# Expert loop of a two-block transformer: the down projection as three products of rounded halves

## The reference, cut to what matters

```
def expert_block(args):
    tok_b, w_b, e = args
    xb = h[tok_b]                                            # 128 x 1024
    hid = jax.nn.silu(xb @ w_e_gate[e]) * (xb @ w_e_up[e])   # 128 x 256
    return (hid @ w_e_down[e]) * w_b[:, None].astype(h.dtype)  # 128 x 1024
```

## Time and profile before

| | |
|---|---|
| median of 3 runs | 3463.89 us (3462.14 to 3467.74) |
| the profiled execution | 3471.0 us, of which its span is 3469.1 us |
| mean granted TensorE clock | 0.978 |
| busy over the span | PE 95%, PEld 74%, DVE 47%, ACT 42%, POOL 38% |
| share of the chain that ended last | PE 79%, DVE 5%, DMA 5%, ACT 4%, issue 4% |

### The profile page before, as it was taken

One profiled execution on the slowest core, in us unless ns is written; L12 is line 12 of the kernel. 1 busy time (PEld: TensorE's weight loads), 2 busy tenths in 40 slices (PEclk: granted clock), 3 DMA queues, 4 the chain that ended last, 5 costly groups with the idle time before them and its releaser, 6 DMA issues.

```text
span 3469.1 us, 44440 instructions
## 1 busy us (share of the span) xinstructions
PE 3280.9 (95%) x17062; PEld 2582.8 (74%) x17062; DVE 1633.8 (47%) x2252; ACT 1455.0 (42%) x1859; POOL 1325.3 (38%) x1076
## 2 busy tenths in 40 slices
PE   7999997899889999999879999998999998899999
PEld 4788886678556666666567888887888877678887
DVE  4555448455576666666543544545311132452121
ACT  4344435522435555555444555555322242342221
POOL 2323137444213333333335444432444443344444
PEclk9999999999999999999989999999999999999999
DMA  5211110244259999999833222221322212032222
GB/s 213 63 50 62 37 49 13 73 178 177 84 205 341 348 343 349 374 359 363 327 121 98 86 80 87 90 86 61 110 97 97 97 50 72 13 109 97 97 97 73
DMA packets 98532, 496.87 MB, mean 143 GB/s; under 512 B 22447, under 2 KB 22703, under 8 KB 49729
## 3 DMA queue, kind: packets, MB, share of 16 engines
q1 hardware_dynamic: 78480, 454.86, 36.8%
q0 software_dynamic: 19888, 39.73, 3.2%
HBM read 472.48 MB, written 40.89 MB: 148 GB/s over the span
## 4 chain that ended last, share of the span: by engine, by line
PE 79%; DVE 5%; DMA 5%; ACT 4%; issue 4%; POOL 2%; SPq 1%; POOLq 0%; ACTq 0%; DVEq 0%
PE ps L283 13%; PE ps L284 13%; PE ps L285 13%; PE ps L2072 7%; DMA arena<-we_gu 4%; PE ps L289 4%; PE ps L291 3%; PE ps L290 3%; PE ps L2057 2%; PE ps L2061 2%; PE ps L2060 2%; PE ps L2610 1%; PE ps L2598 1%; PE ps L705 1%; PE ps L2580 1%
## 5 line engine op out<-in xcount | busy, mean ns | idle before, releaser
L283 PE MATMUL ps<-arena_r,arena_r 128*128 128x512 f32 x2080 | 826.0, 397 | 22.8 <-POOL ring_r L273 6.9
L284 PE MATMUL ps<-arena_r,arena_r 128*128 128x512 f32 x2080 | 815.1, 392 | 0.0
L273 POOL TENSOR_TENSOR ring_r<-ring,arena_r 128x512 fp32r<-128x512 f32 x400 | 554.6, 1418 | 654.3 <-ACT arena_r L268 654.3
L268 ACT ACTIVATE arena_r<-ring 128x2048 fp32r<-128x2048 f32 x166 | 316.7, 1909 | 408.7 <-PE ps L285 331.4
L273 POOL TENSOR_TENSOR arena_r<-ring,arena_r 128x512 fp32r<-128x512 f32 x264 | 335.3, 1302 | 381.0 <-ACT arena_r L268 381.0
L283 PEld LDWEIGHTS ps<-arena_r,arena_r 128*128 128x128 f32 x2080 | 393.2, 189 | 115.2 <-issue 22.6
L284 PEld LDWEIGHTS ps<-arena_r,arena_r 128*128 128x128 f32 x2080 | 393.7, 189 | 81.5 <-issue 1.9
L285 PE MATMUL ps<-arena_r,arena_r 128*128 128x512 f32 x1056 | 410.8, 389 | 0.0
L285 PE MATMUL ps<-arena_r,ring_r 128*128 128x512 f32 x1024 | 403.5, 394 | 0.0
L2160 DVE TENSOR_TENSOR arena_r<-arena,arena_r 128x2048 fp32r<-128x2048 f32 x132 | 301.7, 2287 | 172.2 <-ACT arena_r L2118 172.1
L2118 ACT ACTIVATE arena_r<-arena 128x2048 fp32r<-128x2048 f32 x132 | 250.9, 1910 | 130.2 <-DMA arena<-we_gu 108.1
(11 more groups left out here) (436 smaller groups left out, 5961.1 us busy)
## 6 DMA issues: line engine op xcount, KB each, us to landing
ring<-wstream SPq DMA_DIRECT2D x177, 1024.0 KB, 4.9
arena<-we_gu SPq DMA_DIRECT2D x132, 1024.0 KB, 8.3
arena<-we_down SPq DMA_DIRECT2D x66, 1024.0 KB, 7.5
arena<-arena SPq DMA_DIRECT2D x256, 64.0 KB, 2.0
arena<-ys SPq DMA_DIRECT2D x32, 512.0 KB, 7.2
arena<-wstream SPq DMA_DIRECT2D x24, 512.0 KB, 7.2
arena<-x_t SPq DMA_DIRECT2D x2, 2048.0 KB, 11.8
rope<-wstream SPq DMA_DIRECT2D x8, 512.0 KB, 8.7
```

Source lines behind the costliest of these rows:

```text
L268: act.activation(whalf(c, 0), ring[:, c % NSLOT, :], ACT.Copy).then_inc(sem("chunk_hi"), 1)
L273: ins = pool.tensor_tensor(whalf(c, 1)[:, q:q + 512], ring[:, c % NSLOT, q:q + 512], whalf(c, 0)[:, q:q + 512].bitcast(F32), ALU.subtract)
L283: pe.matmul(out, hi, rhs[0], start=start, stop=False)
L284: pe.matmul(out, hi, rhs[1], start=False, stop=False)
```

## The change

The down product is made like gate and up: ACT rounds the down weights into a buffer of their own (`expert_hi(s, 2)`), DVE writes the remainder over the raw weights, the hidden block too is kept as two halves (`HIDT[s][0]` by ACT, `HIDT[s][1]` by DVE, for both blocks), and PE does three products where there was one. New steps stand at the head of each pair on ACT and DVE. ACT now takes both hidden blocks out of PSUM before `turned` 1. The load of `dmask_flat` moves behind the last pair, since the new buffer overlaps its place. Three semaphores are added and given their start values. The core of the diff:

```
         EW_HI = [[R + 18432 + 4096 * s, R + 20480 + 4096 * s, R + 26624 + 2048 * s] for s in range(2)]
-        HIDT = [view(R + 30720 + 256 * s, 256) for s in range(2)]
+        HIDT = [[rounded(R + 30720 + 512 * s + 256 * part, 256) for part in range(2)] for s in range(2)]
...
             def down(s, j, first_done=None):
                 for k in range(2):
-                    mm = pe.matmul(bank(2 * s + j), HIDT[s][:, k * P:k * P + P], expert_raw(s, 2)[:, k * D + j * 512:k * D + j * 512 + 512],
-                                   start=(k == 0), stop=(k == 1))
+                    hidden = [half[:, k * P:k * P + P] for half in HIDT[s]]
+                    hi, lo = (w[:, k * D + j * 512:k * D + j * 512 + 512] for w in (expert_hi(s, 2), expert_lo(s, 2)))
+                    mm = pe.matmul(bank(2 * s + j), hidden[0], hi, start=(k == 0), stop=False)
                     if first_done is not None and k == 0:
                         mm.then_inc(sem(first_done), 1)
+                    pe.matmul(bank(2 * s + j), hidden[0], lo, start=False, stop=False)
+                    mm = pe.matmul(bank(2 * s + j), hidden[1], hi, start=False, stop=(k == 1))
                 return mm
 
             def down_ready(i, s, back):
                 pe.wait_ge(sem(f"moe_hidt{s}"), i + (1 - back))
-                pe.wait_ge(sem(f"moe_w{s}2"), i * 16 + (16 - 16 * back))
+                pe.wait_ge(sem("moe_d_lo"), i * 2 + (s + 3 - 2 * back))
                 if not back:
                     pe.wait_ge(sem(f"moe_xt{s}"), i + 2)
...
+            def high_down(s, i, back):
+                act.wait_ge(sem(f"moe_w{s}2"), i * 16 + (16 - 16 * back))
+                act.activation(expert_hi(s, 2), expert_raw(s, 2), ACT.Copy).then_inc(sem("moe_d_hi"), 1)
...
             def pair_of_blocks(i, back):
+                high_down(0, i, back)
                 silu(i, 0, back)
+                high_down(1, i, back)
                 if not back:
                     turned(0, i + 2)
                     high(0, 0, i * 16 + 32)
                 silu(i, 1, back)
-                act.wait_ge(sem("moe_hturn"), i * 2 + (3 - 2 * back))
-                act.activation(HIDT[0], bank(6, 256), ACT.Copy).then_inc(sem("moe_hidt0"), 1)
+                for s in range(2):
+                    act.wait_ge(sem("moe_hturn"), i * 2 + (3 + s - 2 * back))
+                    act.activation(HIDT[s][0], bank(6 + s, 256), ACT.Copy).then_inc(sem("moe_hidt_hi"), 1)
                 if not back:
                     turned(1, i + 2)
                     high(0, 1, i * 16 + 32)
...
+            def low_down(s, i, back):
+                dve.wait_ge(sem("moe_d_hi"), i * 2 + (s + 3 - 2 * back))
+                dve.tensor_tensor(expert_lo(s, 2), expert_raw(s, 2), expert_hi(s, 2).bitcast(F32),
+                                  ALU.subtract).then_inc(sem("moe_d_lo"), 1)
+
+            def hidden_low(s, i, back):
+                dve.wait_ge(sem("moe_hidt_hi"), i * 2 + (s + 3 - 2 * back))
+                dve.tensor_tensor(HIDT[s][1], bank(6 + s, 256), HIDT[s][0].bitcast(F32),
+                                  ALU.subtract).then_inc(sem(f"moe_hidt{s}"), 1)
...
             def pair_of_blocks(i, back):
+                low_down(0, i, back)
                 value(i, 0, back)
+                low_down(1, i, back)
                 if not back:
                     turned(0, i + 2)
                     low(0, 0, i * 4 + 5)
                 value(i, 1, back)
+                hidden_low(0, i, back)
+                hidden_low(1, i, back)
                 if not back:
                     turned(1, i + 2)
-                dve.wait_ge(sem("moe_hturn"), i * 2 + (4 - 2 * back))
-                dve.tensor_copy(HIDT[1], bank(7, 256)).then_inc(sem("moe_hidt1"), 1)
                 if not back:
                     low(0, 1, i * 4 + 6)
                     low(1, 0, i * 4 + 7)
...
-            pool.dma_start(dmask_flat, dmask_t[:, 0:4 * TA]).then_inc(sem("dil_loaded"), 16)
             pool.dma_start(dmask_turned, dmask_t[:, 4 * TA:5 * TA]).then_inc(sem("dil_loaded"), 16)
             pool.dma_start(WZ, w_z).then_inc(sem("dil_loaded"), 16)
             pair_of_blocks(n - 1, False)
+            pool.dma_start(dmask_flat, dmask_t[:, 0:4 * TA]).then_inc(sem("dil_loaded"), 16)
```

10 lines of the change are left out of this document (7 added, 3 removed).

## The result

The changed kernel takes 3543.91 us (median of 4 runs, 3538.76 to 3548.04); the kernel before, run beside it, 3465.27 us. The ratio is 1.023, 95% interval 1.0213 to 1.0246: slower by 2.3%, where 3540 us had been forecast. The profiled execution after took 3546.1 us, its span 3544.2 us, at a mean granted clock of 0.971 for 0.978 before.

What follows compares the result with a forecast made beforehand. Before, PE bounded the kernel's pairs, sometimes after late loads; afterwards DVE would. Stage +73 us, first pair +2, last -1, mask +1: +75 on the profiled 3471.0, median 3540 us (range 3508 to 3588).

Steps and rivals of the forecast that it cites:

- DVE paces the pair: Expert stage: DVE's 18.0 us of work and 4.4 us of waits set a 22.4 us period; chance 0.65.
- the two steps: PE waits 2.0 us before down 0, behind `low` (0,0) on DVE, and 1.4 us before down 1, for `turned` 1.
- PE's saving of 1.50 us a pair: Down product on PE: 24 fast products take 5.46 us instead of 6.96, so PE's pair falls to 18.56 us.
- Loads as slow as today: Rival, expert weight loads: period 23.9 us at full clock, 24.4 with clock loss, 3570 us; chance 0.15.
- The clock: PE's pauses halve the clock in about three pairs in ten, 1.8 us each, 0.5 us a pair.
- The rival in which it falls in every pair: Rival, expert stage: the clock drops every pair, 24.4 up to 25.2 us a pair, 3590 us; chance 0.13.
- The row after a pause of 2.13 us: Earlier trace's clock reading: mean 0.67 after that pause; after pauses of 1.65 us it stayed 1.00.
- The stage as a whole: Expert stage: 31 periods at 23.1 for 20.73 us add 73 us; first pair +2 us, last pair -1 us.
- the argument: Down 0 on PE, before needing only ACT's hidden copy, now waits for DVE's `hidden_low` 0 behind `low` (0,0) and `value` 1.
- +1 us there, for the mask: Start of the tail: the later 768 KB mask load meets the gathers on full DMA engines, +1 us (0 to 2).
- The rival on the other side: Rival, expert stage: new steps hide, loads decide at 19.0 to 19.5 us a pair, -47 us, 3417; chance 0.04.
- Signs: Expert stage, if right: DVE busy over 0.8, DMA share well under 0.95; a clock well under 0.9 would show it wrong.

Runs made afterwards that it cites:

- e1: Changed kernel with `value` 1 and `hidden_low` 0 ahead of `low` (0,0) on VectorE; 3492.9 us, ratio 1.0071 to the kernel before.
- e2: Changed kernel with both `turned` 1 steps back ahead of hidden 1 on ScalarE and VectorE; 3515.7 us, ratio 1.0138 to the kernel before.
- e3: Changed kernel with the reorderings of e1 and e2, and `high` (0,1) ahead of hidden 1 on ScalarE; 3490.9 us, ratio 1.0066.
- e6: Changed kernel with down as one plain float32 product instead of three, all new ScalarE and VectorE steps kept; 3570.9 us, ratio 1.0305.
- e5: Changed kernel plus 16 dummy transposes on TensorE in its pause before down 0; 3535.1 us, ratio 1.0194 to the kernel before.
- e8_best: e7 with the remainder of the second down tile moved ahead of `value` 1 on VectorE; 3438.6 us, ratio 0.9919 to the kernel before.
- e7: e3 with the second down tile rounded and its remainder made later, gate/up tile (0,0) after them; 3471.9 us, ratio 1.001.
- e9: e8_best with hidden 1 taken ahead of `high` (0,0) on ScalarE; 3482.7 us, ratio 1.0049 to the kernel before.

## Why the prediction was right

- **DVE paces the pair; 22.4 us undisturbed, 22.6 with the loads.** Measured 22.50, in twelve of 31 periods to a hundredth of a microsecond. PE's pauses, forecast at 2.0 and 1.4 us, are 2.03 and 1.34. e1, e2 and e3 confirm the two steps one by one, with undisturbed periods of 20.8, 21.6 and 19.6 for 20.5, 21.4 and 19.4.
- **PE's saving of 1.50 us a pair.** It is there (starts of the down products 0.23 us apart) and e6 shows that only 0.36 us of it reach the end in this order.
- **Loads as slow as today** (a rival, 1.3 us in every pair): it happened in 4 of 31 pairs, 1.3 to 1.6 us each, just under 0.2 us a pair where 0.2 had been allowed. The reason given holds too: with the longer period `we_gu` lands 6.8 us after its issue in the middle, for 8.4. The rival's price was mis-added: 24.4 us is 3.7 over 20.73, so 31 pairs are 114 us and the kernel 3579, not 105 and 3570; the forecast does not use it.
- **The clock: the mis-sized term.** The sum had three pairs in ten at 1.8 us, 0.5 us a pair. It was 18 of 31 at 1.2 us, 0.7 us a pair: twice the number at two thirds of the cost, two errors that partly cancel. The rival in which it falls in every pair was further off in number and no nearer in cost. The 0.50 of the earlier trace rows follows PE's 3.81 us pause ahead of L2344 at 1732.83 in that trace. The row after a pause of 2.13 us told more than the one after 1.65; e5 shows that the clock is the cause of these long pairs. The rule of the Trainium skill for bursts parted by waits ("TensorE: Matmul & The Clock Gate", section "HAM oscillation — how this bites in real kernels") fits more than half of the pairs, not each one; the page's own case has longer waits.
- **The stage as a whole.** 31 periods: +82 us where +73 was forecast; first pair +2.2 (+2), last -1.5 (-1). The last output copy is 82.7 us later (1774.31 for 1691.64).
- **A slip in the reading.** The hidden copy of block 0 starts at 1415.45 and is made 0.38 us later; `value` 1 starts at 1417.19 all the same, so the argument stands.
- **Behind the stage: an error that happened to help.** I forecast +1 us there, for the mask. The profiled execution after is 7.6 us shorter from the last output copy to its end (1769.9 for 1777.5 us). In the traces of the nine experiments this part takes 1767 to 1775 us with the code of the changed kernel. The long one is that of before, an execution 6 us over its median; that it is an outlier is likely, not shown. So the two profiles together show +75 us as forecast by two errors that cancel, and the medians +79. What lengthens this part from one execution to the next stays open. The cost of the later mask load can't be told from nothing within it; no run tried it apart.
- **The rival on the other side** (the new steps hide, faster) needed DVE's waits to overlap with PE's work. e8_best is that case: same work, another order, 20.05 us a pair. So it was open to this work, and closed only by the order in the diff as written.
- **Signs.** DVE's share of the stage is 0.79, just under the 0.8 named (0.82 in an undisturbed pair); DMA share 0.86; clock 0.96.

## What to carry to other kernels

Where work is moved from a full engine to two that have slack, add up the slack of the receiving engines first, and then write out who stands behind each new step in their fixed order: here 18.4 us of work and 4.1 us of waits a pair on DVE, with the clock and a few late loads on top, turned a saving of 1.5 us on PE into a loss of 2.6, and the same steps in another order were a gain of 0.7. Put a step that needs a late load, or that nobody needs soon, where its engine waits anyway; not ahead of the short steps on which the full engine depends. And look for the pauses that a change gives TensorE: with one of 2.0 us a pair, and with late loads on top, the clock was lower in more than half of the pairs, and with 1.6 us at most (e7, e9) in none.

## What the runs showed of the hardware that I had not expected

**DVE's subtractions hold POOL up.** Groups by line of POOL, 1040 to 1640 us, before and then after (x count | busy us, mean ns): issuing the scatter of the output rows takes 1.01 us before and 2.47 after, and the copy of its indices 1.09 and 1.55, with no change in either.

```profile
L2214 POOL DMA_INDIRECT ys<-arena x58 | 58.8, 1014 | 54.0 <-POOLq L2213 50.4 <-issue 3.6
```

```profile
L2240 POOL DMA_INDIRECT ys<-arena x52 | 128.2, 2466 | 46.0 <-POOLq L2239 46.0
L2237 POOL COPY arena<-arena 128x1 uint32 x51 | 78.9, 1546 | 115.2 <-POOLq L2236 115.2
```

In the timeline after, such a scatter starts on POOL while DVE's two-input subtraction of 1334.02 runs, and ends 0.9 us after it. A copy of one column starts during another such subtraction (1319.66 to 1321.95) and ends with it; the same instruction takes 0.18 us when none runs:

```profile
1320.29 1.70 POOL L1768 COPY arena<-arena 128x1 uint32 x1
...
1326.93 0.18 POOL L1768 COPY arena<-arena 128x1 uint32 x1 [3.01 <-POOLq L2245]
...
1334.43 2.79 POOL L2240 DMA_INDIRECT ys<-arena  x1 [0.89 <-POOLq L2239]
```

It is so throughout the 600 us: the 30 such copies that met no subtraction took 0.18 to 0.19 us, the 73 that started during one 1.1 to 2.0. Of the scatters before none started during a subtraction (1.0 us each), after nearly all did (2.15 to 2.79 us). It cost nothing here, since nobody waits for POOL in time, but an indirect DMA on a critical path would have got 1.5 us longer by a change on another engine.

**A clock that falls for 2 us pauses, but not each time.** At 1348.68 it was half after a pause of 2.04 us, at 1326.18 full after one of 2.03. Two periods alike in work and order differ by 1.5 us through it, and 16 dummy transposes are cheaper than the loss. In the eleven traces together, 341 periods, each of the 65 with a lower clock has a PE pause of 1.93 us or more; so have 36 with the full clock, one of them a pause of 3.44 us. What decides between the two stays open.
